# Block two's mixer anew: convolution taps as diagonal products on TensorE, attention between the projections

## The reference, cut to what matters

```python
def second_block(x, ...):
    hn = rms_norm(x, mix_norm_g)
    proj = hn @ w_in                      # 1024 -> q,k,v,gate of each path
    gq, gk, gv, glr, gog, cu, dq, dk, dv = split(proj)
    o_gla  = gla_mixer(gq, gk, gv, glr, gog, ...)      # gated linear attention, 4 heads
    o_conv = conv_mixer(cu, conv_w, conv_b, ...)       # 31 taps, 256 channels
    o_diff = diff_attention(dq, dk, dv, ...)           # 4 heads, two maps each
    x = x + concat([o_gla, o_conv, o_diff]) @ w_out
    x = x + hier_moe(rms_norm(x, ffn_norm_g), ...)

# gla: b is the running sum of log decays along time
#   state_t = exp(g_t) * state_(t-1) + k_t v_t ;  o_t = q_t state_t
#   scores_ij = sum_d q_id k_jd exp(b_id - b_jd) for j <= i
# conv: z = a * sigmoid(gate); y_t = bias + sum_w z_(t-30+w) * conv_w[w], each channel
#   by itself; then group norm over 64 channels, silu
# diff: a = softmax(q1 k1) - lambda softmax(q2 k2); o = a v, norm per head
```

## Time and profile before

| | us |
|---|---|
| median of 3 runs (1217.83 to 1220.76) | 1218.12 |
| the profiled execution, its own time | 1220.84 |
| its span, first to last instruction | 1219.0 |
| TensorE products busy | 1157.4 (95%) |
| TensorE weight loads busy | 1051.9 (86%) |
| VectorE busy | 831.6 (68%) |
| ScalarE busy | 677.9 (56%) |
| GpSimd busy | 133.2 (11%) |

### The profile page before, as it was taken

How to read it: one execution, slowest core, us unless ns; L and a number is a source line. 1 busy time by engine, 2 the same in 40 slices (tenths; PEclk the granted TensorE clock), 3 DMA queues, 4 the chain that set the end, 5 groups by cost and what they waited for, 6 DMA issues and landing times.

```text
span 1219.0 us, 21118 instructions
## 1 busy us (share of the span) xinstructions
PE 1157.4 (95%) x7756; PEld 1051.9 (86%) x7756; DVE 831.6 (68%) x1375; ACT 677.9 (56%) x1174; POOL 133.2 (11%) x169
## 2 busy tenths in 40 slices
PE   8999899999999999979999999999887899899998
PEld 8998888899999899968889999988886688788886
DVE  6766555877777795655477777785955558557995
ACT  7654244755555776423575555576732454547784
POOL 0002510000000000161000000004791000000000
PEclk9999899999999999999999999999896598999999
DMA  7543102465565364400146656543331016657992
GB/s 247 176 152 122 36 1 87 138 200 185 179 188 187 126 190 147 147 36 1 51 133 194 189 182 190 174 145 131 122 105 52 1 35 215 235 190 258 355 351 89
DMA packets 49799, 181.10 MB, mean 149 GB/s; under 512 B 5568, under 2 KB 5728, under 8 KB 49600
## 3 DMA queue, kind: packets, MB, share of 16 engines
q1 hardware_dynamic: 48816, 176.98, 44.2%
q0 software_dynamic: 912, 3.16, 0.8%
HBM read 179.07 MB, written 1.05 MB: 148 GB/s over the span
## 4 chain that ended last, share of the span: by engine, by line
PE 85%; DVE 6%; POOL 4%; ACT 3%; issue 1%; DMA 1%; DVEq 0%; SPq 0%; ACTq 0%; POOLq 0%
PE bank L1662 22%; PE bank L1664 22%; PE bank L1663 22%; PE bank L1900 2%; PE bank L1889 2%; PE bank L1746 2%; PE bank L1898 2%; PE bank L1722 1%; PE bank L1730 1%; POOL region L1605 1%; PE bank L1713 1%; POOL region L1580 1%; POOL region L1583 1%; PE bank L1752 1%; PE bank L1751 1%
## 5 line engine op out<-in xcount | busy, mean ns | idle before, releaser
L2274 DVE TENSOR_TENSOR w<-ring,w 128x1024 fp32r<-128x1024 f32 x234 | 287.8, 1232 | 107.9 <-ACT w L2013 107.8
L1662 PE MATMUL bank<-act,w 128*128 128x256 f32 x1216 | 349.0, 287 | 13.0 <-DVE w L2274 6.3
L1664 PE MATMUL bank<-act,w 128*128 128x256 f32 x1216 | 344.9, 284 | 0.0
L1663 PE MATMUL bank<-act,w 128*128 128x256 f32 x1216 | 344.8, 284 | 0.0
L2013 ACT ACTIVATE w<-ring 128x1024 fp32r<-128x1024 f32 x234 | 246.2, 1053 | 68.4 <-PE bank L1664 65.2
L1662 PEld LDWEIGHTS bank<-act,w 128*128 128x128 f32 x1216 | 234.0, 192 | 17.1 <-issue 11.7
L1663 PEld LDWEIGHTS bank<-act,w 128*128 128x128 f32 x1216 | 234.2, 193 | 2.1
L1664 PEld LDWEIGHTS bank<-act,w 128*128 128x128 f32 x1216 | 234.0, 192 | 0.0
L2566 DVE SCALAR_TENSOR_TENSOR region<-bank,pf,region 128x255 f32<-128x255 f32 (+1 forms) x176 | 84.8, 482 | 36.4 <-ACT region L2231 25.5
L1662 PE MATMUL bank<-w,hid 128*128 128x512 f32 x206 | 81.7, 397 | 0.0
L1663 PE MATMUL bank<-w,hid 128*128 128x512 f32 x206 | 81.5, 395 | 0.0
(11 more groups left out here) (422 smaller groups left out, 2196.2 us busy)
## 6 DMA issues: line engine op xcount, KB each, us to landing
ring<-wtiles SPq DMA_DIRECT2D x234, 512.0 KB, 3.5
ring<-etiles SPq DMA_DIRECT2D x33, 512.0 KB, 5.1
act_raw<-etiles SPq DMA_DIRECT2D x33, 512.0 KB, 5.1
sq<-etiles SPq DMA_DIRECT2D x22, 512.0 KB, 5.0
cst<-etiles SPq DMA_DIRECT2D x8, 512.0 KB, 5.1
region<-packp POOLq DMA_DIRECT2D x4, 512.0 KB, 4.0
cst<-consts SPq DMA_DIRECT2D x1, 1348.0 KB, 11.4
x<-xt SPq DMA_DIRECT2D x2, 512.0 KB, 5.7
```

Source lines behind the costliest of these rows:

```text
L1662: t.matmul(out_, still[:, 0], moving[:, 0], start=first, stop=False)
L1663: t.matmul(out_, still[:, 0], moving[:, 1], start=False, stop=False)
L1664: return t.matmul(out_, still[:, 1], moving[:, 0], start=False, stop=last)
L2274: v.tensor_tensor(w_lo[:, s, :], ring[:, s, :], w_hi[:, s, :].bitcast(F32), ALU.subtract).then_inc(lo_ready, 1)
```

## The change

Block one's code is left alone, but for clears: the zeroing of block two's tables, which GpSimd did at block two's start, now stands in block one's last feed-forward part. In block two:

- 48 of the 62 taps (all 31 of j=1, 17 of j=0) become matrix products by diagonal matrices. They come as six more weight tiles of eight 128x128 diagonals each, through the same ring and the same halves. The moving operand is `c_z`, shifted by the tap, split into high and low. VectorE keeps 14 taps of j=0. GpSimd has none.
- the pair work has GpSimd no longer. VectorE subtracts, multiplies by q and by k in four pieces of 4 query places each, with 4, 8, 12 and 16 keys (256 to 1024 elements each). The pieces hold entries outside the triangle too, so ScalarE clips by Relu before each Exp.
- the between-block tables are multiplied in three operations in place of 15.
- the steps: the loop has 28. q and k of the softmax attention are projected at 6 to 13, the output gate at 14 and 15, values at 16 to 19, 21 and 22; tap tiles stand at 20 and 23 to 27. The unit factors are all spread at the end of step 15, and the 8 score maps are done at steps 16 to 23, with turns and values at 20 to 26.
- the output product runs in the order linear attention, softmax attention, convolution; the norms of the latter two stand between its tiles, and its last three tiles do the first half of the positions before the second, with two of four groups of x transposes ahead of the last piece.

```diff
+U_CONV, U_DQ, U_OG, U_DVA, U_GV, U_DVB, U_STEPS = 2, 6, 14, 16, 18, 21, 28
+TAP_TILES = 6
+U_TAPS = (20, 23, 24, 25, 26, 27)[:TAP_TILES]
...
-POOL_TAPS = (4, 10, 24)
-SPREAD_STEPS = (16, 17, 20)
+U_SCORES, U_WITHIN = 18, 20
+KI_STEPS = {7: (1, 4), 8: (4, 6), 12: (6, 10), 13: (10, 13), 14: (13, NGB)}
+BETWEEN = ((1, 6), (6, 11), (11, NGB))
+TAPS_AT = {9: 1, 10: 1, 17: 1, 19: 1, 23: 1, 24: 1, 25: 4, 26: 2}
+TURN_STEPS, VALUE_STEPS, LENGTH_STEPS = (20, 22, 24, 25), (21, 23, 25, 26), (26, 26, 26, 27)
+MIX_ORDER_2 = (0, 1, 4, 5, 6, 7, 2, 3)
...
+                elif u in U_TAPS:
+                    if u == U_TAPS[0]:
+                        pe.wait_ge(cz_low, 2)
+                        pe.wait_ge(st_copied, 2)
+                    tile_in(n)
+                    for i in range(KD):
+                        tap = U_TAPS.index(u) * KD + i
+                        j, w = PE_TAPS[tap]
+                        first, last = w == 0, tap == len(PE_TAPS) - 1 or PE_TAPS[tap + 1][0] != j
+                        out_, weights = bank[5][:, j * S:(j + 1) * S], wblock(n % SLOTS, i)
+                        t.matmul(out_, weights[:, 0], cz_hi[:, j, w:w + S], start=first, stop=False)
+                        t.matmul(out_, weights[:, 0], cz_lo[:, j, w:w + S], start=False, stop=False)
+                        mm = t.matmul(out_, weights[:, 1], cz_hi[:, j, w:w + S], start=False, stop=last)
+                    mm.then_inc(tile_done, 1)
...
+                if u == U_DVA - 1:
+                    pe.wait_ge(dn_inv, 1)
+                    for at, i in enumerate(UNITS):
+                        spread(bank[(6, 7, 4, 5)[at // 2]][:, at % 2 * S:at % 2 * S + S], d_inv[:, 4 * i:4 * i + 4], 2).then_inc(dn_row, 1)
+                i = u - U_DVA
+                if 0 <= i < 8:
+                    if i >= 2:
+                        pe.wait_ge(df_sm, i - 1)
+                    if i % 4 == 0:
+                        pe.wait_ge(dn_ready, 4 + i)
+                    scores(i, d_raw[:, 0:4, :], d_raw[:, 4:8, :], bank[6 + i % 2]).then_inc(df_s, 1)
...
+            out_part(0)
+            pe.wait_ge(hn_inv, 2)
+            pe.wait_ge(cy_ready, 2)
+            for j in range(DFH):
+                spread(bank[4 + j // 2][:, j % 2 * S:j % 2 * S + S], o_inv[:, 2 * j:2 * j + 2]).then_inc(hn_row, 1)
...
+            for c in range(NT):
+                for i in range(KD - SLOTS, KD):
+                    if (c, i) == (NT - 1, KD - 1):
+                        x_turn(0)
+                        x_turn(1)
+                    out_part(i, (c,))
...
+            def pair_decay(g):
+                part = g_pr[:, 4 * g:4 * g + 4, :].rearrange("p r (b j) -> p r b j", j=GB)[:, :, :, 0:4 * g + 4]
+                act.wait_ge(pr_sub, g + 1)
+                a.activation(part, part, ACT.Relu).then_inc(pr_pos, 1)
+                act.wait_ge(pr_pos, g + 1)
+                a.activation(part, part, ACT.Exp, scale=-1.0).then_inc(pr_exp, 1)
...
+            def between_blocks(g):
+                lo, hi = BETWEEN[g]
+                dve.wait_ge(ge_ready, (2, 4, 5)[g])
+                keys = slice(0, (hi - 1) * GB)
+                ins = v.tensor_tensor(g_ki[:, lo - 1:hi - 1, keys], g_ki[:, lo - 1:hi - 1, keys],
+                                      g_k[:, keys].unsqueeze(1).to_broadcast([P, hi - lo, (hi - 1) * GB]), ALU.mult)
...
+            def pairs_b(g):
+                v.tensor_tensor(pair_part(g), by_key(g_b, g), by_query(g_b, g), ALU.subtract).then_inc(pr_sub, 1)
+            def pairs_q(g):
+                dve.wait_ge(pr_exp, g + 1)
+                v.tensor_tensor(pair_part(g), pair_part(g), by_query(g_q, g), ALU.mult).then_inc(pr_q, 1)
+            def pairs_k(g):
+                dve.wait_ge(pr_q, g + 1)
+                v.tensor_tensor(pair_part(g), pair_part(g), by_key(g_k, g), ALU.mult).then_inc(pr_ready, 1)
```

More of the change, by code:

```diff
@@ L652, in second_tensor @@
                 if u == 3:
+                    pe.wait_ge(lam_ready, 1)
+                    t.matmul(bank[6][:, 0:2], ones[0:64, :], lam_p[0:64, :], start=True, stop=True).then_inc(lam_sum, 1)
                     pe.wait_ge(lr_ready, 1)
@@ new lines, in second_tensor @@
+                if u in TURN_STEPS:
+                    j = TURN_STEPS.index(u)
+                    pe.wait_ge(df_pn, j + 1)
+                    if j == 0:
+                        pe.wait_ge(u_evac, evacuated(U_GV + 1))
+                    else:
+                        pe.wait_ge(df_pt, j)
+                    for i in range(3):
+                        mm = transpose(bank[3][:, i * P:(i + 1) * P], d_prob[:, 2 * j, i * P:(i + 1) * P])
+                    mm.then_inc(df_t, 1)
+                if u == U_WITHIN + 5:
+                    pe.wait_ge(go_sq, 2)
+                    for j in range(2):
+                        mm = lengths(bank[4][:, 4 * j:4 * j + 4], g_sq[:, j, :], halves)
+                    mm.then_inc(hn_sum, 1)
@@ L723, in second_tensor @@
                     mm.then_inc(hn_row, 1)
-                if i == 3:
-                    pe.wait_ge(cy_ready, 1)
-                    for j in range(2):
-                        mm = t.matmul(bank[5][:, j * S:(j + 1) * S], bd64, c_y[:, j, :], start=True, stop=True)
-                    mm.then_inc(cm_done, 1)
-                if i == 6:
-                    pe.wait_ge(csq_ready, 2)
-                    for j in range(2):
-                        mm = lengths(bank[5][:, 4 * j:4 * j + 4], c_sq[:, j, :], halves)
-                    mm.then_inc(hn_sum, 1)
@@ L758, in second_tensor @@
-                j, odd = divmod(i - 5, 2)
-                if 0 <= j < DFH and odd == 0:
-                    if j == 0:
-                        pe.wait_ge(gla_mix, 1)
-                    pe.wait_ge(df_o, 2 * j + 2)
-                    mm = lengths(bank[4][:, 2 * j:2 * j + 2], d_osq[:, j, :], ones[:, 0:1])
-            mm.then_inc(hn_sum, 1)
-            pe.wait_ge(hn_inv, 2)
-            for j in range(2):
-                mm = spread(bank[5][:, j * S:(j + 1) * S], c_inv[:, 4 * j:4 * j + 4], 2)
@@ L781, in second_tensor, with out_part, x_turn @@
+            def out_part(i, both=range(NT)):
+                k, n = MIX_ORDER_2[i], T2 + U_WOUT + i
+                if 0 in both:
+                    tile_in(n)
+                    pe.wait_ge(mix_lo, DEPTH * KD + i + 1)
+                token_product(SECOND_SUMS, act_both[:, :, k, :], n % SLOTS, i == 0, i == KD - 1, both)
             XT_BANKS = (0, 1, 4, 5)
-            for i in range(2 * NT):
+            def x_turn(i):
                 c, j = divmod(i, 2)
```

639 lines of the change are left out of this document (326 added, 313 removed).

## The result

The changed kernel took 1205.63 us (median of four runs, 1203.93 to 1210.25), against 1219.44 for the kernel before (four runs, 1217.83 to 1220.83): 0.9893 of its time, 95% interval 0.986 to 0.9926, or 13.8 us less. Timed again later beside other kernels it took 1205.00 us, 0.9873 (0.9856 to 0.989). The forecast was 1202, in a range of 1193 to 1214.

What follows compares the result with a forecast made beforehand. TensorE's waits and attention at the lower clock were taken as the losses. Mixer -20.2, after it -1.3, clock +5.0: -16.5 us from the profiled 1220.84 gives 1204.3, 1201.6 for the median, put as 1202 us; range 1193 to 1214.

Steps and rivals of the forecast that it cites:

- the stretch: Block two's mixer, first projection to last output product: 179.4 us before, forecast 159.2 us without the added clock cost.
- the three falls: Granted clock dropping in two runs of 4-column sums (steps 20, 21) and the wait before the output: 1.6 to 1.7 us each.
- the fall behind the gated value: Lower clock after TensorE's 2.3 us wait for the gated convolution value, expected to keep costing 1.6 us.
- the 149.6 of the sum: TensorE's work in block two's mixer at upper clock: dense tiles 106.0 us plus small products 43.6 us.
- Rival B: Weight-half ring falls behind beside attention on VectorE and ScalarE, +10 us over the 12 last steps: 1212 us; chance 0.17.
- rival C: Unaligned operands double the tap tiles, or these replace waiting with equal work: +17 us, 1218, no change; chance 0.05.
- the clock's term: Cost of three short drops of TensorE's granted clock in block two's mixer, put at +5.0 us.
- the one at 845: Old kernel's lower clock from 845 to 848 us, behind the gated-value wait; its 1.6 to 1.7 us priced the new drops.
- a sign of being wrong: Prediction called itself wrong if the granted clock in block two's mixer stayed at 0.50 for more than 15 us.
- Rival D: Lower clock holds from step 16 to the output, some 67 us at half rate: about 1230 us, slower; chance 0.06.
- The tail: Behind the last output product, transposes and a residual row half already done save some 1.3 us.
- the largest added term: Six tap tiles on TensorE in block two's mixer, 2.9 us each, 17.3 us on the path.

Runs made afterwards that it cites:

- e1: Changed kernel with the 32 within-block sums given 64 columns of moving operand in place of 4: 1201.88 us, ratio 0.9852 to the kernel before.
- e2: Changed kernel with the 4-column within-block sums put two at a time between the value tiles' products, in place of runs of 16: 1202.08 us, ratio 0.9847.
- e9: Changed kernel without tap tiles, taps dealt out anew on VectorE, sums 64 columns wide, mix parts and first gate's sigmoid earlier: 1191.39 us, ratio 0.9768.
- e11: Changed kernel with the last three output tiles multiplied whole and all x transposes behind the last product, as in the old kernel: 1205.47 us, ratio 0.9872.
- e8: Changed kernel with no tap tiles, VectorE doing all 62 taps, three or four to a step: 1197.84 us, ratio 0.9818 to the kernel before.
- e7: Changed kernel with the softmax attention moved behind all projections and tap tiles, in twelve added steps: 1213.79 us, ratio 0.9945 to the kernel before.
- e6: Changed kernel with within-block sums 64 columns wide, mix parts before the last tap tile's refill, and first gate's sigmoid one step earlier: 1194.53 us, ratio 0.9786.

## Why the prediction was right, and where not

**Direction and size.** 1205.63 for 1202, with -13.8 us for -16.5. For the stretch the forecast was 159.2 us and 5.0 for the clock, 164.2; measured were 166.85.

**The sum without the three falls was right.** The three falls cost 3.4, 3.4 and 1.7 us by the rows shown (each microsecond there times one minus its clock), 8.5 together. What is left of the stretch is 158.3 us, for 159.2; both hold the fall behind the gated value, forecast at 1.6 us and 1.7 by its rows. TensorE's busy time less what all four falls cost is 149.5 us, for the 149.6 of the sum. The tap tiles took 2.9 us each, 3.10 from first start to last end; the spreads waited 1.1 for the forecast 1.2, the first output product 3.5 for 3.3, the gated value 2.3, and no low half was waited for. Rival B (a ring that falls behind) and rival C (unaligned operands) had their signs named, and both are absent: no wait for a low half, 0.28 to 0.29 us for each tap product.

**The step that was mis-sized is the clock's term**, 8.5 us for 5.0: three falls were placed rightly, but each was priced by the one at 845, 1.6 to 1.7 us. The two within the narrow sums lasted 7 us and cost 3.4 each. The row that would have served is another: the fall that the earlier trace rows show beginning at 1005 lasted in the old kernel to 1012.5 and cost 3.4 us as well. I had priced a fall behind a wait, and these were falls within a run of narrow products. e1 and e2 show that the run is what they follow. With the fall behind the gated value the clock was at 0.50 for some 20 us in sum, over the 15 us that the prediction had named as a sign of being wrong; no single fall came near 15, so it depends on how that sign is read.

**Rival D** (the lower clock holds for good) did not come: dense tiles brought the clock back each time. e9 shows that stretch without dense tiles, 17 us at 0.52.

**VectorE** was put at 6 us less, and came out 10.2 less, 101.4 for 111.6. Its wide passes take 3.1 to 3.2 us each and the three between-block products 2.9, as worked out:

```profile
L1327 DVE TENSOR_TENSOR region<-region 128x256 f32<-128x256 f32 (+3 forms) x4 | 3.2, 818 | 0.0
L1290 DVE TENSOR_TENSOR region<-region 128x400 f32<-128x400 f32 (+2 forms) x3 | 2.9, 965 | 0.0
L1269 DVE SCALAR_TENSOR_TENSOR region<-region,pb 128x256 f32<-128x256 f32 x13 | 6.2, 477 | 0.2
```

Of the further 4.2 us, the taps that stayed are 1.7: they cost 0.477 in place of 0.609 beside GpSimd, a saving that the prediction had in its price of 0.48 and left out of its sum. The other 2.5 were not traced. It made no difference, because VectorE was not the bound: it waits 50.5 us for high halves.

```profile
DVE w L2352 <- ACT w L2091: 50.5, 25, 6.9
```

**The tail**, -1.3 us for the split output, is not confirmed (e11). -2.2 us in the profile are within what the same code does by itself.

**What the prediction did not ask** is whether the largest added term should have been paid at all. It called VectorE "not a bound if the queue order is good" and still let the tap tiles' 17.3 us stand as the price of relieving it. The walk showed 1 to 3 us to spare nearly everywhere with 14 taps left; e8 shows that all 62 fit. By the waits that are gone, what made the change faster is the rest of it: GpSimd out of the decays and the taps, with the 8.3 and the 5.7 us waits that hung on its chain and on the narrow tables' place in the queue, and the attention between the tiles, worth 9 us (e7, the only one of these that was undone by itself; the share of GpSimd is argued from the waits and not shown).

**On headroom**: matmul idle time gave the change 7 us at most, weight-load idle time 22. It came to 12.5 in the stretch, between them. The changed kernel then had 7.1 us of matmul idle time and 18.8 of weight-load idle time (148.0 busy of 166.85), and e6, with the same dense work, took 13.3 us more out of the stretch. So matmul idle time is no upper bound, and that agrees with the Trainium skill (Perfetto Trace Analysis, Identifying the Most-Contended Engine), which does not judge TensorE's headroom by it. But the trace does not show weight loads to be the better measure: from the changed kernel to e6, matmul busy time fell by 9.1 us and weight-load busy time by 8.8. Most of the gain, 10.2 us by its rows, came from the clock, which is 1.00 throughout in e6, and the lower clock lengthens both: from 909 to 915 us in the changed kernel each shows 6.00 of 6.00 us busy.

## What to carry to other kernels

Before work is moved to the engine that sets the end, give it back on paper to the engine that had it, with a better order in its queue: here the kernel without the move was 7 us faster than the one with it. A run of products with very few columns between dense tiles is worth widening or dealing out among the dense ones, which gave 5 to 6 us of the stretch here. When a stretch is made up of waits of several us, look at what the late step is queued behind: two of three such waits went by moving one or two instructions a step ahead.

## What the runs showed of the hardware that was not expected

- 32 records of 4 columns in a row take 3.6 us at full clock (908.00 in the earlier trace rows). In the new order the clock falls to 0.50 within each such run or up to 1.1 us behind it, for 3.5 to 7 us and once for 10 (e8); with 64 columns they take 3.79 us and the clock is 1.00 throughout; with 4 columns, by twos between 256-column products, it is 1.00 as well.
- Tap products, every second of them with a moving operand that begins at an odd element, take 281 to 291 ns, like the aligned ones (288), and start at an even pace of 0.12 us.
- The clock falls at some places in one execution and not in the next of the same kernel: behind the 2.3 us wait it fell in the first profile of the changed kernel and not in the second, 1.4 us of the stretch.
- With the attention alone (e7) the falls cost 10.2 us more by the clock's rows than in the changed kernel, and TensorE was busy 7.3 us longer: narrow products feel the lower clock too, in good part.
